# Gate and value chunks of three feed-forwards with x's high and low part as one 512-column operand

## The reference

```python
h = rms_norm(x, norm_ffn_pre[layer])
u = h @ w_up[layer].astype(h.dtype)
u = causal_depthwise_conv(u, ffn_conv_w[layer], ffn_conv_b[layer])   # 3 taps
u_gate, u_val = jnp.split(u, 2, axis=-1)
f = jax.nn.gelu(u_gate, approximate=True) * u_val
y = f @ w_down[layer].astype(f.dtype)
x = x + rms_norm(y, norm_ffn_post[layer])
```

```python
x = x + 0.5 * ((jax.nn.silu(h @ w1) * (h @ w3)) @ w2)     # h = rms_norm_2(x, g)
```

## Time and profile before

| | |
|---|---|
| three runs | 1134.72, 1135.49, 1132.76 us (median 1134.72) |
| profiled execution: span | 1134.3 us, 0.4 us below the median of the runs |
| PE busy | 1113.6 us, 98% of the span, 9558 matmuls |
| DVE busy | 769.0 us, 68% |
| ACT busy | 559.7 us, 49% |
| POOL busy | 183.4 us, 16% |
| L2173 to L2175, their share of the chain that ended last | 21%, 20%, 20% |
| feed-forward 0, 1, 2 | about 299 to 487, 497 to 678, 949 to 1123 us |

### The profile page before, as it was taken

The page is one execution under the profiler, slowest core; times in us unless marked ns, Lnnn a source line. Parts: engine busy times, 40 slices in busy tenths (PEclk is TensorE's granted clock), DMA queues, the critical chain, the costliest instruction groups (busy, mean ns, idle before and its releaser), DMA issues.

```text
span 1134.3 us, 22063 instructions
## 1 busy us (share of the span) xinstructions
PE 1113.6 (98%) x9558; PEld 1054.5 (93%) x9558; DVE 769.0 (68%) x1032; ACT 559.7 (49%) x671; POOL 183.4 (16%) x128
## 2 busy tenths in 40 slices
PE   8999999999999999999999999999999999999997
PEld 7999999899899999889999999999999989999996
DVE  4888978757687767776456467984368675564564
ACT  6433344484665545574334348723244656343343
POOL 3898783000000000000000010113030000000000
PEclk9999999999999999999999999999999999999999
DMA  8586553355366555545655564423134454655551
GB/s 267 190 268 216 186 186 112 112 180 186 115 217 207 184 185 185 185 130 192 191 193 174 192 189 149 149 77 114 40 117 146 147 166 162 211 179 190 188 180 41
DMA packets 147149, 190.00 MB, mean 167 GB/s; under 512 B 7659, under 2 KB 132139, under 8 KB 146943
## 3 DMA queue, kind: packets, MB, share of 16 engines
q1 hardware_dynamic: 145743, 184.32, 50.0%
q0 software_dynamic: 1264, 4.55, 1.2%
q10 hardware_dynamic: 64, 0.02, 0.0%
HBM read 187.79 MB, written 2.65 MB: 168 GB/s over the span
## 4 chain that ended last, share of the span: by engine, by line
PE 91%; DVE 3%; ACT 3%; issue 1%; DMA 0%; SPq 0%; ACTq 0%; DVEq 0%
PE bank L2173 21%; PE bank L2174 20%; PE bank L2175 20%; PE bank L2318 6%; PE bank L2319 6%; PE bank L2320 6%; PE bank L584 2%; PE bank L653 1%; DVE w_lo L1754 1%; PE bank L2252 1%; PE bank L558 1%; ACT sq L1475 1%; PE bank L2455 1%; PE bank L2201 1%; ACT w_hi L1461 0%
## 5 line engine op out<-in xcount | busy, mean ns | idle before, releaser
L2173 PE MATMUL bank<-X_hi,w_hi 128*128 128x256 f32 x1760 | 502.2, 285 | 0.4 <-DVE w_lo L1754 0.2
L2174 PE MATMUL bank<-X_lo,w_hi 128*128 128x256 f32 x1760 | 497.9, 283 | 0.0
L2175 PE MATMUL bank<-X_hi,w_lo 128*128 128x256 f32 x1760 | 497.9, 283 | 0.0
L1461 ACT ACTIVATE w_hi<-w_raw 128x2048 fp32r<-128x2048 f32 x170 | 324.0, 1909 | 149.8 <-PE bank L2175 113.4
L1754 DVE TENSOR_TENSOR w_lo<-w_raw,w_hi 128x2048 fp32r<-128x2048 f32 x144 | 332.5, 2311 | 43.6 <-ACT w_hi L1461 43.3
L2173 PEld LDWEIGHTS bank<-X_hi,w_hi 128*128 128x128 f32 x1760 | 337.4, 192 | 6.0 <-issue 2.6
L2174 PEld LDWEIGHTS bank<-X_lo,w_hi 128*128 128x128 f32 x1760 | 337.5, 192 | 1.1
L2175 PEld LDWEIGHTS bank<-X_hi,w_lo 128*128 128x128 f32 x1760 | 337.5, 192 | 0.0
L1881 DVE TENSOR_TENSOR arena<-bank,rstd 128x512 f32<-128x512 f32 x66 | 45.6, 691 | 184.0 <-PE bank L2175 179.3
L1370 POOL TENSOR_TENSOR w_lo<-w_raw,w_hi 128x2048 fp32r<-128x2048 f32 x23 | 106.7, 4648 | 35.2 <-ACT w_hi L1461 35.2
L2318 PE MATMUL bank<-w_hi,Y_hi 128*128 128x512 f32 x264 | 103.3, 391 | 1.2 <-DVE Y_lo L1909 1.2
(11 more groups left out here) (300 smaller groups left out, 1398.7 us busy)
## 6 DMA issues: line engine op xcount, KB each, us to landing
w_raw<-in_ffn_w_dram SPq DMA_DIRECT2D x66, 1024.0 KB, 5.3
w_raw<-in_w_in_dram SPq DMA_DIRECT2D x52, 1024.0 KB, 5.1
w_raw<-in_w_up_dram SPq DMA_DIRECT2D x22, 1024.0 KB, 5.1
w_raw<-in_w_down_dram SPq DMA_DIRECT2D x11, 1024.0 KB, 5.0
w_raw<-in_w_out_dram SPq DMA_DIRECT2D x8, 1024.0 KB, 4.9
w_raw<-in_conv_pw_w_dram SPq DMA_DIRECT2D x4, 1024.0 KB, 5.1
w_raw<-in_w_attn_out_dram SPq DMA_DIRECT2D x2, 1024.0 KB, 5.1
w_raw<-in_rwkv_proj_dram SPq DMA_DIRECT2D x2, 1024.0 KB, 4.7
```

The lines of the kernel that those rows point to most:

```text
L1461: a.activation(w_hi[slot][:, :], raw[slot][:, :], ACT.Copy).then_inc(S["w_hi"], told.one("w_hi"))
L2173: pe.matmul(o, wh, xh, start=start, stop=False, skip_group_check=True)
L2174: pe.matmul(o, wh, xl, start=False, stop=False, skip_group_check=True)
L2175: return pe.matmul(o, wl, xh, start=False, stop=stop, skip_group_check=True)
```

## The change

In pairs 1 to 10 the gate and val chunks are done by `by_columns_wide`: one matmul of 512 columns moves x_hi and x_lo together (they lie in one tensor, `X_both`, 2048 columns apart) against w_hi, and writes a whole bank, the product with x_hi in its first half and the one with x_lo in its second; one of 256 columns adds w_lo times x_hi to the second half. A chunk so needs two banks, one per tile m: gate uses banks 2 and 3, val banks 0 and 1. Pair 0 and, in feed-forward 0, val 10 stay as they were. ACT copies the second halves to SBUF (`low_sums`), DVE adds the first halves to the copy instead of multiplying by `rstd`, and POOL multiplies by `rstd`: in feed-forward 0 gate and value, in 1 and 2 the gate and then silu's result. The consumers wait for POOL's signal `scaled`. Three signals of the mixer are merged into others.

```diff
+            def feed(k):                                  # GpSimd
+                for i in range(1, FPAIRS):
+                    pool.wait_ge(S["gate_read"], FPAIRS * k + i + 1)
+                    gate = u_t[:, 0].rearrange("p (m t) -> p m t", m=2)
+                    g.tensor_tensor(gate, gate, over(rstd[:], 2), ALU.mult).then_inc(
+                        S["scaled"], told.one("scaled"))
+                    if k == 0 and i < FPAIRS - 1:
+                        pool.wait_ge(S["val_read"], i + 1)
...
+                    if k > 0:
+                        pool.wait_ge(S["act_gate"], FPAIRS * k + i + 1)
+                        gate = act_t.rearrange("p (m t) -> p m t", m=2)
...
+                def low_sums(side, i):                    # ScalarE
+                    if k == 0 and side == 1 and i == FPAIRS - 1:
+                        return
+                    act.wait_ge(S["chunk_used"], b0 + 3 * i + side)
+                    a.activation(low_t[:, side].rearrange("p (m t) -> p m t", m=2),
+                                 side_banks[1 - side][:, :, T:2 * T], ACT.Copy).then_inc(
+                        S["low_copied"], told.one("low_copied"))
...
                 for i in range(1, FPAIRS - 1):
+                    low_sums(1, i)
+                    split(b0 + 3 * i + 3)
                     val_part(i)
-                    split(b0 + 3 * i + 3)
                     f_part(i)
                     split(b0 + 3 * i + 4)
+                    low_sums(0, i + 1)
+                    split(b0 + 3 * i + 5)
                     gate_part(i + 1)
-                    split(b0 + 3 * i + 5)
+                low_sums(1, FPAIRS - 1)
...
+                    else:                                 # VectorE, evacuate
+                        dve.wait_ge(S["low_copied"], low_count(k, side, i))
+                        v.tensor_tensor(o, side_banks[1 - side][:, :, 0:T],
+                                        low_t[:, side].rearrange("p (m t) -> p m t", m=2), ALU.add).then_inc(
+                            S[name], told.one(name))
...
+            def by_columns_wide(n, slot, side):           # TensorE
+                split_ready(n)
+                for k in range(NT):
+                    for m in range(2):
+                        c = k * 256 + m * P
+                        o = side_banks[1 - side][:, m, :]
+                        pe.matmul(o.rearrange("p (a t) -> p a t", a=2), w_hi[slot][:, c:c + P], X_both[:, :, k, :],
+                                  start=k == 0, stop=False, skip_group_check=True)
+                        mm = pe.matmul(o[:, T:2 * T], w_lo[slot][:, c:c + P], X_hi[:, k, :], start=False,
+                                       stop=k == NT - 1, skip_group_check=True)
+                mm.then_inc(S["chunk_used"], told.one("chunk_used"))
```

More of the change, by code:

```diff
@@ L321, in block_pair, with low_count, scaled_count @@
         act_t, f_t = region(2048, 2 * T), region(2560, 2 * T)
+        low_t = region(3072, 2, 2 * T)
+        WIDE = FPAIRS - 1
+        def low_count(k, side, i):
+            return 2 * WIDE * k - (k > 0) + 2 * (i - 1) + side + 1
+        def scaled_count(k, second, i):
+            return 2 * WIDE * k - (k > 0) + 2 * (i - 1) + second + 1
         token_gain = region(8192, D)
@@ L799, in act_mixer @@
             split(B0 + 4)
-            for ready, b, dst, gain, done in (("decay_in", 6, dec, "rwkv_w0_2", "decay_read"),
-                                              ("rate_in", 4, rate, "rwkv_a0_2", "rate_read")):
-                act.wait_ge(S[ready], 1)
+            act.wait_ge(S["low_rank_up"], 1)
+            for b, dst, gain, done in ((6, dec, "rwkv_w0_2", "decay_read"), (4, rate, "rwkv_a0_2", "rate_read")):
                 for t in range(HT):
@@ L1406, in _ @@
                 pool.dma_start(lora_w[row:row + k, part, :], ap[0]).then_inc(S["lora_landed"], 16)
+            def feed(k):
[6 more added lines that the diff above has]
+                        pool.wait_ge(S["val_read"], i + 1)
+                        val = u_t[:, 1].rearrange("p (m t) -> p m t", m=2)
+                        g.tensor_tensor(val, val, over(rstd[:], 2), ALU.mult).then_inc(
+                            S["scaled"], told.one("scaled"))
+                    if k > 0:
+                        pool.wait_ge(S["act_gate"], FPAIRS * k + i + 1)
+                        gate = act_t.rearrange("p (m t) -> p m t", m=2)
+                        g.tensor_tensor(gate, gate, over(rstd[:], 2), ALU.mult).then_inc(
+                            S["scaled"], told.one("scaled"))
+            feed(0)
+            feed(1)
             def low_of(n):
@@ L1444, in _ @@
             low_of(LOW_BY_POOL[1])
+            feed(2)
         @block.scalar
@@ L2350, in body @@
                     else:
-                        pe.wait_ge(S["val_read"], i + before)
-                    by_columns(at + 3, b0 % RING, 2 * (1 - parity) + 1)
+                        pe.wait_ge(S["gate_read"], i + (before + 1))
+                    by_columns_wide(at + 2, (b0 + 2) % RING, 0)
+                    if first and i == 0:
+                        pe.wait_ge(S["gate_read"], before + 1)
+                    pe.wait_ge(S["val_read"], i + (before + 1))
+                    if narrow_val:
+                        by_columns(at + 3, b0 % RING, 0)
+                    else:
+                        by_columns_wide(at + 3, b0 % RING, 1)
                     pe.wait_ge(S["f_lo"], i + (before + 1))
```

69 lines of the change are left out of this document (42 added, 27 removed).

## The result

| | median of 5 runs | lowest to highest | span of the profiled execution |
|---|---|---|---|
| before | 1134.63 us | 1132.44 to 1135.49 | 1134.3 us |
| after | 1142.51 us | 1141.72 to 1143.69 | 1142.0 us |

The ratio is 1.0073, with a 95% interval of 1.0062 to 1.0084: slower by 7.9 us (0.7%), above the range of 1127 to 1141. The profiled execution of after took 1143.69 us with a span of 1142.0, so 1.7 us lie around the span; in the other runs it is 1.7 to 2.0.

What follows compares the result with a forecast made beforehand. PE's own pace was taken to bound the kernel. The terms -12.3 + 8.8 + 3.1 + 0.8 gave +0.4 us on a span of 1134.3, hence a median of 1135 us, range 1127 to 1141.

Steps and rivals of the forecast that it cites:

- PE's part: Wide chunks of all feed-forwards: a step falls from 0.360 to 0.347 us, -12.3 us over 59 chunks.
- the third rival: Wide matmuls: the two-piece operand costs its start twice, 1143; decides from 0.007 us extra per matmul; 7%.
- The chain of 17.5 us: Feed-forward 0, each pair: closed chain through DVE, POOL and ACT exceeds PE's 16.56; waits cost +8.8 us.
- the first rival: POOL's scaling starts only after DVE's low part and takes its full 1.31 us or more: 1138 to 1140; 15%.
- the estimate of 0.115 + 1.31: POOL's hand-over after DVE's low part by the skill's page: 1.43 us instead of 1.15, 5 us more, 1140.
- The second rival: Feed-forward 0: POOL gets in before DVE's low part or runs beside it, period 15.5, total 1123; 10%.
- The first pair: Start of feed-forward 0's pairs: the first of nine PE waits is some 0.4 us longer than the others' 0.93.
- The wait before down 10: End of feed-forward 0: PE waits 4.3 us for the last f instead of 1.2, +3.1 us.
- a small rival: After feed-forward 0: the longer wait may bring a half-clock stretch, +1.7 us; no chance of its own given.
- Ends of feed-forwards 1 and 2: Last low part of f comes at 11.4 against 11.0 needed: +0.4 us each, +0.8 in all.
- The base: The span of 1134.3 us to which the changes were added, with the median taken 0.4 above it.

Runs made afterwards that it cites:

- e1: The changed kernel with x's high and low part of each step side by side in SBUF: 1142.57 us.
- e12: The changed kernel with feed-forward 0 as before; in 1 and 2 all 16 wide matmuls of a chunk precede its 16 narrow ones: 1126.01 us.
- e14: The changed kernel with all wide matmuls of a chunk first, DVE scaling in feed-forward 0 and its last pair narrow: 1122.37 us.
- e5: The changed kernel, but in feed-forward 0 DVE waits for POOL's scaling before its low part: 1135.66 us.
- e2: The changed kernel with the two wide matmuls of each step k before the two narrow ones: 1139.14 us (one run).
- e4: The changed kernel without POOL's scaling by rstd in feed-forward 0: 1130.46 us (one run).
- e10: The changed kernel with wide and narrow matmuls grouped two by two and DVE instead of POOL scaling in feed-forward 0: 1127.56 us.
- e6: The changed kernel, but DVE itself multiplies by rstd in feed-forward 0, without POOL: 1129.99 us.
- e3: The changed kernel with feed-forward 0 put back as before the change: 1130.71 us.
- e9: The changed kernel with feed-forward 0 as before and, in 1 and 2, matmuls grouped two wide, two narrow: 1126.28 us.
- e13: The changed kernel with matmuls grouped two by two, DVE scaling in feed-forward 0 and its whole last pair narrow: 1123.26 us.
- e15: The changed kernel with feed-forward 0 as before; in 1 and 2 sizes alternate but neighbouring matmuls write different banks: 1129.70 us (one run).

## Why the prediction was wrong

The prediction's mechanism stands. The sizes of some of its terms do not, and the largest miss is in the part that it took for the safest. Of the 7.15 us between the forecast of the span (+0.45) and what was found (+7.6), PE's pace in feed-forwards 1 and 2 (with what lies between) makes 4.7, the ends of the two -0.8, the pairs of feed-forward 0 2.2 and the clock 1.05.

1. **The failed step: "PE's part".** It took the wide matmul at nothing above the 512-column row, a step of 0.347. The step was 0.353, and the period of feed-forwards 1 and 2 fell by 0.19 instead of 0.42. On their 40 wide chunks that is a gain of 20 x 0.19 = 3.8 us where 40 x 0.21 = 8.3 was written. With their ends and what lies between, -7.5 was forecast and -3.6 came. In feed-forward 0 the slower step shows hardly at all, since the chain bound it anyway. The reason given ("the columns and the output are those of the 512-column row") holds for a stream of such matmuls: e1 shows that the two pieces cost nothing, and e12 and e14 show both paces as read. What was not asked is what the *mixture* does. The earlier trace rows show streams of one size only, and the trace of before has no stretch in which the sizes alternate. The price at which it decides, 0.007 per wide matmul, was written under the third rival. That price, 0.006 to 0.007, is what was paid, for another cause; that the number agrees is luck.
2. **The chain of 17.5 us.** 17.59 measured, and not by luck: the three parts were written as 6.85, 6.94 and 3.70 and measured 6.88, 6.96 and 3.75, with POOL's end 1.15 after the low part, as taken. PE's waits in the pairs are shorter than the 0.9 forecast (17.59 - 16.79 = 0.80), because PE is slower. The late hand-over of the first rival did not happen, nor the estimate of 0.115 + 1.31 that the prediction had worked out by the Trainium skill (SBUF — State Buffer, "A bandwidth-pool intuition that's wrong"), whose figure was taken on a DMA's descriptors. The exclusive lock of the same page of the Trainium skill ("Who interferes with whom") agrees with the traces: the operation's record is 3.27 us behind the low part and 1.30 ahead of it (e5). The second rival, no lock, is refuted by the same records.
3. **The first pair.** It was given one wait, some 0.4 longer than the others. It had two, for the low parts of gate 2 and of val 2 (1.02 and 1.18 us): the first distance is 19.38, 1.8 above a period. That is 1.5 us more than forecast. The 0.09 per period over the following eight make another 0.7. These two are the 2.2 of the pairs, but for tenths.
4. **The wait before down 10.** 4.16 us against 4.3. Right.
5. **The half clock behind it.** 6.8 us at 0.50 (1.2 GHz), +2.55 on the last down, where the prediction named +1.7 as a small rival. It began during the 4.16 us of waiting, in which PE did nothing. e1 and e2, with the same wait, had 6.8 us as well (e1 3.4 us more a little later). In the other traces the length of the wait does not order it: 3.4 us of half clock in e4 (waiting 1.9) and e10 (2.7), none at this place in e5 (3.4) and e6 (2.7), nor in e3, e9, e12, e13, e14 and e15 (1.2 to 1.5). A trace is one execution: by the mean clocks, e5's was one of the four faster ones of ten. No run changed the wait alone. The half clock of before at 295.9, which after lacks, gives some 1.5 back; e3, e9, e12 and e15, whose code up to there does the same work as before's, lack it, so it may be of that one execution.
6. **Ends of feed-forwards 1 and 2.** +0.4 each forecast, and nothing there: 5.50 for the last two downs against 5.47.
7. **The base.** 1134.3 was taken as 0.4 below the median; with 1.7 us around each span it was 1.4 above it. This moves no difference of spans, only the comparison with the medians: spans of +7.6, medians of +7.9.

The balance of the spans, forecast against found: feed-forwards 1 and 2 -7.5 against -3.6; feed-forward 0, its last down left out, +7.95 against +10.15 (the 10.35 of the table and 0.2 saved in the two wide chunks ahead of down 0); the clock 0 against +1.05 (-1.5 and +2.55). That is +0.45 against +7.6.

## What to carry to other kernels

A stream's price is a property of the order as well as of its instructions. Where a change mixes two sizes of matmul that the trace shows only apart, keep each size together (grouping by two was enough here, 0.2 us per 32 steps), and put a cost on the mixture in the forecast. Where GpSimd and a VectorE operation with two SBUF inputs meet, the order decides who pays. Let the short one go first, or keep the operation on VectorE when that has the time to spare. Then look at the last pair, whose chain nothing covers.

## What the runs showed of the hardware

- 512- and 256-column matmuls in turn, each with its own weight load, take 0.353 us a pair instead of 0.228 + 0.120, in nearly all chunks. Behind a pause the same code sometimes runs at 0.347, and keeps that pace until the next pause or down chunk.
- Grouped two by two a pair takes 0.348 (e2, e9), sixteen by sixteen 0.347 (e12, e14).
- The moving operand's two pieces of 256 columns, NT x 256 columns apart, cost nothing against adjacent ones (e1).
- A GpSimd operation of 1.30 us that arrives 0.16 us after a VectorE low part of 2.28 us ends 1.15 us after it, less than its own length.
- PE's wait of 4.2 us, entered at full clock, turned into 6.8 us at half clock in all three traces that had it.
